# Expert blocks of a two-layer decoder: ACT's and DVE's work in another order round the up projection, low halves awaited later, two semaphores for an expert's weights

## The reference

```python
gate = p_top * top_p / jnp.sum(top_p, axis=-1, keepdims=True)   # two experts a token
padded = (counts + MOE_BLOCK - 1) // MOE_BLOCK * MOE_BLOCK       # blocks of 128 rows
def run_block(args):
    xb, e = args
    hid = jax.nn.silu(xb @ w_gate[e]) * (xb @ w_up[e])
    return hid @ w_down[e]
y = jax.ops.segment_sum(out[dest] * sw[:, None].astype(out.dtype), stok, num_segments=T)
```

## Time and profile before

| what | value |
|---|---|
| median of 3 runs | 3131.38 us |
| lowest and highest | 3124.84, 3132.12 us |
| the profiled execution's own time | 3119.75 us |
| its span, first to last instruction | 3117.8 us |
| PE busy | 2673.4 us, 86% of the span |
| PEld, DVE, ACT, POOL busy | 2236.8, 1747.1, 1260.4, 724.0 us |
| mean granted clock of PE | 0.936 of full speed |
| moved by DMA | 509.57 MB, 163 GB/s on average |

### The profile page before, as it was taken

One profiled execution on the slowest core, in us unless ns is written; L12 is line 12 of the kernel. 1 busy time (PEld: TensorE's weight loads), 2 busy tenths in 40 slices (PEclk: granted clock), 3 DMA queues, 4 the chain that ended last, 5 costly groups with the idle time before them and its releaser, 6 DMA issues. The chain is left out here.

```text
span 3117.8 us, 48627 instructions
## 1 busy us (share of the span) xinstructions
PE 2673.4 (86%) x15109; PEld 2236.8 (72%) x15112; DVE 1747.1 (56%) x3154; ACT 1260.4 (40%) x2369; POOL 724.0 (23%) x923
## 2 busy tenths in 40 slices
PE   5999979997968947998898599799879947989997
PEld 4999958875847836777676488578658836767775
DVE  4222246665755665667765366588733354676664
ACT  3222132225841104556654222288611104675653
POOL 1000023321110002444343143211100002444433
PEclk9999989998988968999999799899979968999998
DMA  6111112215536516899997322222154415999995
GB/s 243 50 56 52 40 60 78 75 65 165 163 121 234 194 61 216 261 301 302 316 281 228 118 87 80 91 83 88 53 198 143 149 39 179 298 359 285 283 308 132
DMA packets 175389, 509.57 MB, mean 163 GB/s; under 512 B 53800, under 2 KB 81456, under 8 KB 150320
## 3 DMA queue, kind: packets, MB, share of 16 engines
q1 hardware_dynamic: 142480, 393.69, 34.7%
q0 software_dynamic: 32800, 114.51, 15.4%
HBM read 374.56 MB, written 133.56 MB: 163 GB/s over the span
## 5 line engine op out<-in xcount | busy, mean ns | idle before, releaser
L1700 DVE TENSOR_TENSOR moe_parts<-expert_w,moe_parts 128x1024 fp32r<-128x1024 f32 x384 | 452.3, 1221 | 238.4 <-ACT moe_parts L1649 234.9
L1582 PE MATMUL ps<-moe_parts,moe_xT 128*128 128x512 f32 x2232 | 551.6, 403 | 23.0 <-issue 16.0
L1582 PEld LDWEIGHTS ps<-moe_parts,moe_xT 128*128 128x128 f32 x2232 | 418.1, 191 | 125.3 <-issue 20.5
L1649 ACT ACTIVATE moe_parts<-expert_w 128x1024 fp32r<-128x1024 f32 x384 | 373.3, 1047 | 80.3 <-PEq L155 78.8
L1109 PE MATMUL ps<-out_w,out_catT 128*128 128x512 f32 x1344 | 322.4, 399 | 14.2 <-DVE out_w L1265 11.8
L560 PE MATMUL ps<-in_gate_w,in_gate_hnT 128*128 128x384 f32 (+1 forms) x1536 | 319.4, 367 | 7.4 <-DVE in_gate_w L679 7.4
L1582 PE MATMUL ps<-moe_parts,moe_hidT 128*128 128x512 f32 x1116 | 289.0, 408 | 26.9 <-DVE moe_hidT L1713 24.2
L560 PEld LDWEIGHTS ps<-in_gate_w,in_gate_hnT 128*128 128x128 f32 x1536 | 278.7, 190 | 37.4 <-issue 7.5
L1109 PEld LDWEIGHTS ps<-out_w,out_catT 128*128 128x128 f32 x1344 | 255.7, 192 | 69.4 <-DVE out_w L1265 12.6
L560 PE MATMUL ps<-in_qk_w,in_qk_hnT 128*128 128x512 f32 x1152 | 268.4, 394 | 9.2 <-DVE in_qk_w L679 9.2
L1582 PEld LDWEIGHTS ps<-moe_parts,moe_hidT 128*128 128x128 f32 x1116 | 205.7, 191 | 76.2 <-DVE moe_hidT L1713 32.8
(11 more groups left out here) (262 smaller groups left out, 4150.8 us busy)
## 6 DMA issues: line engine op xcount, KB each, us to landing
expert_w<-in_w_gate SPq DMA_DIRECT2D x64, 1024.0 KB
expert_w<-in_w_up SPq DMA_DIRECT2D x64, 1024.0 KB
expert_w<-in_w_down SPq DMA_DIRECT2D x64, 1024.0 KB
hn_d<-out_hn SPq DMA_DIRECT2D x32, 512.0 KB, 2.6
in_gate_xt<-in_x SPq DMA_DIRECT2D x16, 512.0 KB
in_qk_xt<-in_x SPq DMA_DIRECT2D x16, 512.0 KB
att_k<-k_d SPq DMA_DIRECT2D x64, 128.0 KB, 2.9
out_ht<-in_x SPq DMA_DIRECT2D x16, 512.0 KB, 4.6
```

The lines of the kernel that those rows point to most:

```text
L1582: last = nc.tensor.matmul(out, left[:, a, k, :], right(b, k), start=(n == 0 and k == 0), stop=(n == 2 and k == K_ - 1))
L1649: nc.scalar.activation(parts[:, j, 0, at], K.expert_w[:, j, at], ACT.Copy).then_inc(w_high.sem, 1)
L1700: nc.vector.tensor_tensor(parts[:, j, 1, at], K.expert_w[:, j, at], parts[:, j, 0, at].bitcast(F32), ALU.subtract).then_inc(w_low.sem, 1)
```

## The change

- **Order on ACT and DVE.** A block's code on the two engines now begins with `act(m-1)` and `hidden(m-1)`, and `x_out(m)` follows, where it ended with `act(m)`, `hidden(m)` and `x_out(m+1)` before. In a first block the splits are spread: one up piece ahead of `x_out`, one behind it, then `y_scaled(m-2)` (ACT) and the expert's own two down pieces, then the next expert's last two up pieces. The down pieces of an expert are split in its own first block, not in that of the one before.
- **Low halves later.** PE waits for `x_high` and `h_high` ahead of a product, and for `x_low` and `h_low` ahead of its third term. `lower` does two terms for both halves of its output first.
- **Signals apart.** `expert_in` becomes `up_in` and `down_in`, `w_high`/`w_low` become `gu_high`, `gu_low`, `d_high`, `d_low`. SP loads the down weights of `e+1` once those of `e-1` are split, then gate and up of `e+2`.
- **Gather.** It takes its indices from `K.where` with a bounds check, so that padding has an index past the last token; `xg` is cleared once at the start. `K.who` is gone.
- **Gates.** ACT reads the gate's column from `K.gates` (one column of zeros ahead), and POOL's copy `set_gate` is gone. ACT makes one y more at the start, which is not scattered.

```diff
@@ -1283,19 +1283,20 @@
             log(end.plus(1))
 
 
-def load_expert(K, sp, layer, e, slot, until_free=lambda n: None):
-
-    nc = K.nc
+def load_up(K, sp, layer, e, slot, until_free=lambda n: None):
+
     for n, name in enumerate(("w_gate", "w_up")):
         until_free(n)
         src = K.x[name][layer].rearrange("e (p k) f -> e p (k f)", k=DK)
         src = src[e] if isinstance(e, int) else src[bass.ds(e, 1)].rearrange("a p f -> (a p) f")
-        dst = K.expert_w[:, slot, n * DK * FF:(n + 1) * DK * FF]
-        sp.dma_start(dst, src).then_inc(K.expert_in[layer][slot], 16)
-    until_free(2)
+        sp.dma_start(K.expert_w[:, slot, n * DK * FF:(n + 1) * DK * FF], src).then_inc(K.up_in[layer][slot], 16)
+
+
+def load_down(K, sp, layer, e, slot):
+
     src = K.x["w_down"][layer].rearrange("e (p k) n -> e p (k n)", k=2)
     src = src[e] if isinstance(e, int) else src[bass.ds(e, 1)].rearrange("a p n -> (a p) n")
...
@@ -1456,8 +1457,8 @@
             v.wait_ge(gathered, 1)
             do(V.tensor_copy(found[:, :, :], table))
 
-            own_.mark(V.tensor_copy(K.who[:, :], found[:, 1, :]))
-            own_.mark(V.tensor_copy(K.gates[:, :], found[:, 2, :]))
+            own_.mark(V.memset(K.gates[:, 0:1], 0.0))
+            own_.mark(V.tensor_copy(K.gates[:, 1:1 + NBMAX], found[:, 2, :]))
             do(V.tensor_scalar(found[:, 0, :], found[:, 0, :], -1.0, 1.0, ALU.mult, ALU.add))
...
@@ -1520,39 +1519,49 @@
         def _(sp):
             def load(i, j):
 
-                load_expert(K, sp, layer, i * 2 + j, j, lambda n: alone(
-                    sp, w_low, i * (2 * PIECES) + ((j - 2) * PIECES + (n + 1) * PIECES // 3), K.tick_sp))
-            with sp.Fori(1, NE // 2) as i:
+                if not (isinstance(i, int) and i == 0 and j == 0):
+                    alone(sp, Count(d_low), (i * 2 + j) * D_PIECES, K.tick_sp)
+                    load_down(K, sp, layer, i * 2 + j + 1, 1 - j)
+                load_up(K, sp, layer, i * 2 + j + 2, j, lambda n: alone(
+                    sp, Count(gu_low), (i * 2 + j) * GU_PIECES + (n + 1) * GU_PIECES // 2, K.tick_sp))
+            for j in range(2):
+                load(0, j)
+            with sp.Fori(1, NE // 2 - 1) as i:
                 for j in range(2):
                     load(i, j)
+            alone(sp, Count(d_low), (NE - 2) * D_PIECES, K.tick_sp)
+            load_down(K, sp, layer, NE - 1, 1)
             if layer == 0:
 
-                sp.wait_ge(w_low.sem, NE * PIECES)
+                sp.wait_ge(gu_low, NE * GU_PIECES)
+                sp.wait_ge(d_low, NE * D_PIECES)
...
             def gather(m):
-                nc.gpsimd.tensor_copy(who[:, :], K.who[:, m:m + 1] if isinstance(m, int) else K.who[:, bass.ds(m, 1)]).then_inc(who_set.sem, 1)
+                nc.gpsimd.tensor_copy(who[:, :], K.where[:, m:m + 1] if isinstance(m, int) else K.where[:, bass.ds(m, 1)]).then_inc(who_set.sem, 1)
                 alone(g, who_set, m + 1, K.tick)
                 nc.gpsimd.indirect_dma_start(xg[:, :], None, K.hn_d[layer],
-                                             bass.IndirectOffsetOnAxis(ap=who[:, :], axis=0)).then_inc(gathered_s, 16)
-
-            def set_gate(m):
-                nc.gpsimd.tensor_copy(gate[:, :], K.gates[:, bass.ds(m, 1)]).then_inc(gated.sem, 1)
+                                             bass.IndirectOffsetOnAxis(ap=who[:, :], axis=0),
+                                             bounds_check=T - 1, oob_is_err=False).then_inc(gathered_s, 16)
 
...
+            g.memset(xg[:, :], 0.0).then_inc(cleared, 1)
+            g.wait_ge(cleared, 1)
             gather(0)
 
...
             with g.Fori(1, total) as m:
-                set_gate(m - 1)
-
                 alone(g, x_turned, m + 2, K.tick)
                 gather(m + 2)
                 scatter(m - 1)
-            set_gate(total - 1)
...
         def _(pe):
-            def product(out, left, right, K_):
-
-                for n, (a, b) in enumerate(((0, 0), (0, 1), (1, 0))):
+            def product(out, left, right, K_, terms):
+
+                for a, b in terms:
                     for k in range(K_):
-                        last = nc.tensor.matmul(out, left[:, a, k, :], right(b, k), start=(n == 0 and k == 0),
-                                                stop=(n == 2 and k == K_ - 1))
+                        last = nc.tensor.matmul(out, left[:, a, k, :], right(b, k), start=(a + b + k == 0),
+                                                stop=(a == 1 and k == K_ - 1))
                 return last
...
             def raise_(m, j):
 
                 wgu = parts[:, j, :, 0:GU].rearrange("p h (s k f) -> p h k s f", s=2, k=DK)
+                until(pe, x_high, m + 1)
+
+                until(pe, hid_done, m)
+                product(gup, xT, lambda h, k: wgu[:, h, k, :, :], DK, ((0, 0), (0, 1)))
                 until(pe, x_low, m + 1)
-
-                until(pe, hid_done, m)
-                product(gup, xT, lambda h, k: wgu[:, h, k, :, :], DK).then_inc(up.sem, 1)
+                product(gup, xT, lambda h, k: wgu[:, h, k, :, :], DK, ((1, 0),)).then_inc(up.sem, 1)
...
             def lower(m, j):
 
                 wd = parts[:, j, :, GU:EW].rearrange("p h (k n) -> p h k n", k=2)
-                until(pe, h_low, m + 1)
-                until(pe, y_out, m)
-                for half in range(2):
-                    last = product(yp[:, 512 * half:512 * (half + 1)], hidT,
-                                   lambda h, k: wd[:, h, k, 512 * half:512 * (half + 1)], 2)
+                until(pe, h_high, m + 1)
+                until(pe, y_out, m + 1)
+                for terms in (((0, 0), (0, 1)), ((1, 0),)):
+                    if terms[0][0] == 1:
+                        until(pe, h_low, m + 1)
+                    for half in range(2):
+                        last = product(yp[:, 512 * half:512 * (half + 1)], hidT,
+                                       lambda h, k: wd[:, h, k, 512 * half:512 * (half + 1)], 2, terms)
                 last.then_inc(down.sem, 1)
...
-                pe.wait_ge(w_low.sem, i * (2 * PIECES) + j * PIECES + GU_PIECES)
+                pe.wait_ge(gu_low, i * (2 * GU_PIECES) + (j + 1) * GU_PIECES)
                 raise_(m, j)
                 turn_x(m + 1)
                 if behind:
+                    pe.wait_ge(d_low, i * (2 * D_PIECES) + j * D_PIECES)
                     lower(m - 1, 1 - j)
-                pe.wait_ge(w_low.sem, i * (2 * PIECES) + (j + 1) * PIECES)
-                pe.sem_inc(K.tick_pe, 1)
-
-            def block_(m, j):
+
+            def block_(i, j, m):
                 turn_hid(m - 1)
                 raise_(m, j)
                 turn_x(m + 1)
+                pe.wait_ge(d_low, i * (2 * D_PIECES) + (j + 1) * D_PIECES)
                 lower(m - 1, j)
...
+            def split_up(j, pieces):
                 for n in pieces:
                     at = slice(n * PIECE, (n + 1) * PIECE)
-                    nc.scalar.activation(parts[:, j, 0, at], K.expert_w[:, j, at], ACT.Copy).then_inc(w_high.sem, 1)
+                    nc.scalar.activation(parts[:, j, 0, at], K.expert_w[:, j, at], ACT.Copy).then_inc(gu_high, 1)
+
+            def split_down(i, j):
+                a.wait_ge(K.down_in[layer][j], i * 16 + 16)
+                for n in range(GU_PIECES, GU_PIECES + D_PIECES):
+                    at = slice(n * PIECE, (n + 1) * PIECE)
+                    nc.scalar.activation(parts[:, j, 0, at], K.expert_w[:, j, at], ACT.Copy).then_inc(d_high, 1)
...
             def y_scaled(m):
                 until(a, down, m + 1)
-                until(a, gated, m + 1)
-
-                a.wait_ge(scattered_s, m * 16 + 16)
-                nc.scalar.activation(y[:, :], yp, ACT.Copy, scale=gate[:, 0:1]).then_inc(y_out.sem, 1)
+
+                a.wait_ge(scattered_s, m * 16 + 32)
+                column = K.gates[:, m + 1:m + 2] if isinstance(m, int) else K.gates[:, bass.ds(m + 1, 1)]
+                nc.scalar.activation(y[:, :], yp, ACT.Copy, scale=column).then_inc(y_out.sem, 1)
 
             def first_block(i, j, m, behind, ahead):
                 ni, nj = i + j, 1 - j
+                if behind:
+                    act(m - 1)
                 if ahead:
-
-                    a.wait_ge(K.expert_in[layer][nj], ni * 48 + 48)
-                    if behind:
-                        until(a, up, m)
-                    split(ni, nj, range(GU_PIECES))
-                act(m)
-                x_out(m + 1)
+                    a.wait_ge(K.up_in[layer][nj], ni * 32 + 32)
+                    split_up(nj, (0,))
+                x_out(m)
+                if ahead:
+                    split_up(nj, (1,))
                 if behind:
-                    y_scaled(m - 1)
+                    y_scaled(m - 2)
+                split_down(i, j)
                 if ahead:
-                    split(ni, nj, range(GU_PIECES, PIECES))
-
-            def block_(m, j):
-                act(m)
-                x_out(m + 1)
```

(32 more changed lines are left out.)

65 lines of the change are left out of this document (40 added, 25 removed).

## The result

The changed kernel takes 3132.83 us (median of 20 runs, 3124.59 to 3138.99), against 3124.05 us (3116.28 to 3133.12) for the kernel before in the same session. The ratio of the medians is 1.0028, with a 95% interval of 1.0019 to 1.0038. I had forecast 3095 us, and against the 3131 of the runs first shown that was 1.2% faster; it is 0.3% slower. The profiled execution's span goes from 3117.8 to 3129.9 us.

A forecast was written before the change was run, and what follows sets the result against it. PE (92% busy) and DMA (90%) were close in the expert stages, so only PE's idle time, 113 us lost, could be gained. Terms -18 - 11 - 7 = -36 us against the 3131.38 us median gave 3095 us, range 3046 to 3123.

The forecast's parts named there:

- the other 55 intervals: -11 us: Raise intervals not beginning a layer or following a one-block expert: 10.0 to 9.8 us each, bounds 0 and -25.
- half of the loss: Of the 0.45 us each of 55 intervals lost to gathers beside weights and x_low, half was kept.
- the 36 intervals: Raise intervals that begin a layer or follow a one-block expert: 12.0 to 11.5 us each, -18 us, bounds 0 and -54.
- the cut ring: ACT, DVE and PE waiting for each other, 12.5 us a round; reordering ends it and 24.2 us of hidT waits.
- the low halves: PE asks for x_low and h_low later in its products; the 16 us of issue waits go, with small exceptions.
- the one-block stretches: Where one-block experts follow each other, DMA and the gather's 11.3 us round trip keep intervals near 11.5 us.
- End of layer 0: -7 us: The last gather no longer waits 8.91 us behind w_in_odd; last scatters meet that load instead; range -9 to -3.
- Rivals one and two: DMA replaces the lost waits in full, 3119 us, chance 0.16; weights run ahead, 3047 us, chance 0.10.
- Rival three: Between one-block experts, late up weights hold ACT's x and so PE's raise; 3155 us, chance 0.07.
- Rival four: Bounds check or DVE's pieces delay POOL's index copy and gather issue, up to 1.8 us a gather; 3195 us, chance 0.04.
- slower: Whole kernel slower than before: chance 0.07, against 0.11 for within 0.3% and 0.82 for faster.

The follow-up runs named there:

- late_loads: Changed kernel with gate and up loads held back until DVE has begun the next expert's first block; 3084.29 us, ratio to the kernel before 0.9862 to 0.9897.
- low_only: Kernel before, with PE asking for the low halves only ahead of the third term of raise and down product; 3119.95 us.
- hid_low: Kernel before, with PE asking for low halves only ahead of the third term and hid_out ahead of the up pieces on DVE; 3128.70 us.
- skip_only: Kernel before, with only the padding's rows skipped in the gather (scatter's index, bounds check, cleared tile); 3126.35 us.

## Why the prediction was wrong

- **The step that failed is the term "the other 55 intervals: -11 us".** They went from 549.7 to 582.6 (253.7 + 328.9), +33. The text had the facts: the loads go out together, "that frees the first gather and puts the second one, full now, beside them". The first half came true (27 intervals, -8.5). For the second I kept "half of the loss" of before and set the bounds at 0 and -25: both on the side of a gain. I read the earlier trace rows as a gather that shares bandwidth with weights, and so priced it by bytes. The trace of before had the evidence for another price, which I didn't look for: from 1253.87 to 1257.0 the gather did not share, it stood still. Behind some 1.5 MB of weights the turn shown then waited 1.22 us; behind the three loads it waits 2.62. late_loads, with the same bytes and the loads behind the gather, takes the whole of it away. Not all of the +33 is the loads': low_only has +10 in these 55 intervals and hid_low +18 with the loads left spread, as I read it because PE comes sooner to a gather that is no sooner. I had no term for that in these intervals.
- **"-18 us" in the 36 intervals: the size was right, the reason not.** They went from 432.2 to 413.0, at 11.55 each behind one-block experts; I had 414. But I put it on the padding, with the cut ring hidden under the DMA bound. Of the parts alone, skip_only has +6.5 in that class, hid_low -2 and low_only -12, the last from an execution 11.7 us faster than its median. With the new order, skipping the padding is worth 12 of the 16 there. Why the new order can use the freed bytes and the old one can't was not tried.
- **The ring and the low halves.** The waits went, as predicted, and PE's pace without waits went from 9.55 to 9.39. That the gather takes their place in the one-block stretches I had said; low_only shows it in the second blocks too.
- **"End of layer 0: -7 us"** was -2.9: from the last raise to layer 1's first instruction on POOL it took 42.2 us and takes 39.3, the weaker end of the range given. The turn no longer waits 8.91, but the last y waits 14.53 for a scatter that stands behind the 5 MB of `w_in_odd`:

```profile
1708.75 1.04 PE L1596 MATMUL ps<-ident,moe_xg 128*128 128x128 f32 x8
```

```profile
1728.44 1.11 ACT L1681 ACTIVATE moe_y<-ps,gates 128x1024 f32<-128x1024 f32 x1 [14.53 <-DMA h_d<-moe_y,moe_where]
```

- **The rivals.** Rivals one and two had the 55 intervals at 9.95 and 9.6; they took 10.6. Rival three was there (ACT's 23 us a layer) and cost nothing that could be found. Rival four named the right place, the gather's round trip in the intervals that it decides, with the wrong cause: POOL's issue is 1.07 us at the median and its copy 0.19 (1.00 and 0.31 before), and what grew is the time from issue to landing. I gave slower 0.07. A rival "the full gather is issued behind the whole of the next weights" was missing, though my own text describes it.
- **The clock**, which I did not price, is part of the +41. In the fourth row of the windows above the granted clock is 0.63 over the down product, so part of it ran at the lower of TensorE's two levels, 1.2 in place of 2.4 GHz:

```profile
1227.51 1.23 PE L1596 MATMUL ps<-ident,moe_xg 128*128 128x128 f32 x8 [2.81 <-DMA moe_xg<-hn_d,moe_who]
1228.42 4.60 PE L1588 MATMUL ps<-moe_parts,moe_hidT 128*128 128x512 f32 x12
```

This product takes 4.60 us in place of 3.00, right behind a turn that waited 2.81 us. The changed kernel has 18 such slow down products, 25 us over full speed in all, 8 of them with 12 us in second blocks (the one shown stands behind a one-block expert); the kernel before has 4, 5 us, none in second blocks.

The sum by what was measured: -19 in the 36 intervals, +33 in the other 55, -2 outside of them: +12, the difference of the spans.

## What to carry to other kernels

When an edit moves loads, list what each transfer that an engine waits for is queued behind, in bytes, at the time of its issue: the order of issue decided here between no wait and 2.6 us, at equal traffic and a DMA share below 0.9. Bulk loads that have slack belong behind the small transfer that has none; held back like that, they made this kernel 1.2% faster than the kernel before (late_loads, 0.9862 to 0.9897), where the same edit without it made it slower. And a term in which something good and something bad meet needs bounds on both sides of zero.
